# A retention layer whose gate, query and key features are made in pairs by seven block products

## The reference

```
h = rms_norm(x, norm_mix_g[1]);  proj = h @ w_in            # 1024 -> 2048 (q, k) + 2048 (v) + 2048 (g)
q = rotary(q), k = rotary(k) / 16                           # 4 heads of 256
s = (q k^T) * decay (causal);  ret = s @ v                  # v: 4 heads of 512
y = rms_norm(ret, out_g) * silu(g);  x = x + y @ w_out
```

## Time and profile before

| what | us |
|---|---|
| timed runs, median of 3 | 2112.48 (2112.15 to 2113.44) |
| the profiled execution, span of its instructions | 2111.6 |
| TensorE busy | 2094.3 |
| VectorE, ScalarE, GpSimd busy | 1358.7, 1088.4, 1115.7 |

### The profile page before, as it was taken

One profiled execution on the slowest core, in us unless ns is written; L12 is line 12 of the kernel. 1 busy time (PEld: TensorE's weight loads), 2 busy tenths in 40 slices (PEclk: granted clock), 3 DMA queues, 4 the chain that ended last, 5 costly groups with the idle time before them and its releaser, 6 DMA issues.

```text
span 2111.6 us, 29835 instructions
## 1 busy us (share of the span) xinstructions
PE 2094.3 (99%) x11235; PEld 1801.2 (85%) x11235; DVE 1358.7 (64%) x2284; ACT 1088.4 (52%) x1750; POOL 1115.7 (53%) x662
## 2 busy tenths in 40 slices
PE   9999999999999999999999999999999999999999
PEld 7867889889888888888899898888888888899998
DVE  7973786767634445467776684897567325785773
ACT  6564654654433424346546545445877535645642
POOL 3514666874534343435758834655433554838843
PEclk9999999999999999999999999999999999999999
DMA  4203223333322222222232324322212342333232
GB/s 167 70 11 93 97 92 100 101 101 106 119 85 90 85 91 84 92 80 89 92 101 93 117 85 174 110 80 72 78 61 71 91 140 90 100 100 101 90 108 93
DMA packets 57677, 200.69 MB, mean 95 GB/s; under 512 B 6400, under 2 KB 7168, under 8 KB 57280
## 3 DMA queue, kind: packets, MB, share of 16 engines
q1 hardware_dynamic: 56816, 197.46, 29.1%
q10 hardware_dynamic: 720, 1.34, 0.2%
HBM read 194.32 MB, written 4.19 MB: 94 GB/s over the span
## 4 chain that ended last, share of the span: by engine, by line
PE 91%; DVE 6%; issue 2%; ACT 2%; DMA 0%; SPq 0%; DVEq 0%; POOL 0%; ACTq 0%
PE ps L404 21%; PE ps L406 21%; PE ps L405 21%; PE ps L707 6%; PE ps L709 6%; PE ps L708 6%; PE ps L434 2%; PE ps L433 2%; PE ps L432 2%; PE ps L2444 1%; PE ps L1837 1%; DVE SC L1051 1%; DVE X L1024 0%; PE ps L2429 0%; PE ps L2456 0%
## 5 line engine op out<-in xcount | busy, mean ns | idle before, releaser
L382 POOL TENSOR_TENSOR WL<-WS,WH 128x1024 fp32r<-128x1024 f32 (+1 forms) x276 | 652.2, 2365 | 710.4 <-ACT WH L372 709.8
L404 PE MATMUL ps<-H,WH 128*128 128x512 f32 (+2 forms) x1488 | 580.8, 390 | 1.7 <-DVE H L612 1.1
L405 PE MATMUL ps<-H,WH 128*128 128x512 f32 (+2 forms) x1488 | 578.0, 388 | 0.0
L406 PE MATMUL ps<-H,WL 128*128 128x512 f32 (+2 forms) x1488 | 577.9, 388 | 0.0
L372 ACT ACTIVATE WH<-WS 128x1024 fp32r<-128x1024 f32 (+2 forms) x278 | 286.6, 1033 | 296.7 <-PE ps L406 167.1
L404 PEld LDWEIGHTS ps<-H,WH 128*128 128x128 f32 (+1 forms) x1488 | 279.1, 188 | 60.4 <-DVE H L612 2.7
L406 PEld LDWEIGHTS ps<-H,WL 128*128 128x128 f32 (+1 forms) x1488 | 279.0, 187 | 58.2
L405 PEld LDWEIGHTS ps<-H,WH 128*128 128x128 f32 (+1 forms) x1488 | 279.2, 188 | 54.5
L1213 POOL TENSOR_TENSOR WL<-WS,WH 128x512 fp32r<-128x512 f32 x162 | 214.2, 1333 | 197.1 <-ACT WH L830 195.3
L404 PE MATMUL ps<-G,WH 128*128 128x512 f32 x496 | 193.6, 390 | 2.0 <-DVE G L2163 1.4
L707 PE MATMUL ps<-G_long,WH 128*128 128x256 f32 x672 | 191.4, 285 | 2.6 <-DVE X L1024 2.1
(11 more groups left out here) (328 smaller groups left out, 4060.2 us busy)
## 6 DMA issues: line engine op xcount, KB each, us to landing
WS<-in_w SPq DMA_DIRECT2D x337, 512.0 KB, 3.5
WS<-in_w SPq DMA_DIRECT2D x24, 384.0 KB, 3.1
xs<-X SPq DMA_DIRECT2D x1, 2048.0 KB, 6.7
X<-xs SPq DMA_DIRECT2D x8, 256.0 KB, 3.7
out<-X SPq DMA_DIRECT2D x8, 256.0 KB, 2.0
X<-in_sg SPq DMA_DIRECT2D x1, 1344.0 KB, 6.0
X<-in_x ACTq DMA_DIRECT2D x4, 256.0 KB, 6.0
X<-in_x SPq DMA_DIRECT2D x4, 256.0 KB, 5.8
```

Of the source, the lines that this page charges most:

```text
L382: e.tensor_tensor(lo, raw, hi.bitcast(F), ALU.subtract).then_inc(*P.sig("w_lo", i))
L404: e.matmul(out, lh, rh, start=start, stop=False)
L405: e.matmul(out, lh, rl, start=False, stop=False)
L406: return e.matmul(out, ll, rh, start=False, stop=stop)
```

## The change

Of the retention's 32 gate, query and key features, 28 are made in pairs of seven products: 8 gate pairs, and the query pair and the key pair of heads 1 to 3. The query and key features of head 0 stay (units `bqk` 0, 1, 8, 9). Ahead of the heads, ScalarE scales X by the norm's weights, GpSimd makes the turned rows of the retention, ScalarE their high part and VectorE their low part. The scores stand around the pairs: two scores, the first gate pair, two scores, the second gate pair. ScalarE makes the forms' high parts, GpSimd the low parts; the weight sums are VectorE's for the gate and query pairs and GpSimd's for the key pairs.

```diff
+R_PAIRS = [("bg", i) for i in range(8)] + [("qk", i) for i in range(2, 8)]
...
-    for m in range(16):
+    for m in (0, 1, 8, 9):
...
-        u["bg", m] = [("b_w_in", 0, k, 4096 + 128 * m, 128) for k in K8]
+    for pair in R_PAIRS:
+        m1, m2 = (r_columns(pair) + 128 * z for z in range(2))
+        u["rp", *pair, 0] = [("b_w_in", 0, k, c, 128) for c in (m1, m2) for k in range(0, 8, 2)]
+        u["rp", *pair, 1] = [("b_w_in", 0, k, c, 128) for c in (m2, m1) for k in range(1, 8, 2)]
...
+def pe_row_pair(P, e, pair, amid=None, hold=False):
...
+    left, right, chain = a[:, 0:256], a[:, 256:512], b[:, 0:256]
+
...
+    pe_product(P, e, pair, "a11", "w_lo", chain, rows(0, 0), True)
+    if pair == ("bg", 0):
+        e.wait_ge(*P.at("t_lo", ("r", 3)))
+    pe_product(P, e, pair, "s1", "w_lo", right, turned("t1"), True)
+    e.wait_ge(*P.at("ct", (pair, "p1")))
+    pe_product(P, e, pair, "s2", "w_lo", chain, turned("t2"), False)
+    e.wait_ge(*P.at("ct", (pair, "p5")))
+    pe_product(P, e, pair, "a12", "w_lo", left, rows(1, 0), False)
+    if amid:
+        amid()
+    e.wait_ge(*P.at("ct", (pair, "u2")))
+    pe_product(P, e, pair, "s3", "w_lo", chain, turned("t3"), False)
+    pe_product(P, e, pair, "s4", "w_lo", right, rows(1, 1), False)
+    e.wait_ge(*P.at("c22", pair))
+    pe_product(P, e, pair, "a22", "w_lo", chain, turned("t4"), False)
+    P.cell_n += 1
+
+
...
-            feature(P, e, ("bg", 4 * h + j), P.hs())
+            if j % 2:
+                pe_row_pair(P, e, ("bg", 2 * h + j // 2))
...
+            q, k = (("qk", 2 * (h + 1) + part) for part in range(2))
+            pe_row_pair(P, e, q, row, True)
+            pe_row_pair(P, e, k)
+            for key in r_keys(q):
+                drop(P, key)
...
     e.preload_act_table_set("natural_log_exp_and_others")
     act_row_split(P, e, "nm1", 7)
-    qk_casts(0, 0)
+    cast(("bqk", 0))
+    cast(("bqk", 1))
     act_row(P, e, "nm1")
+    scaled(0)
+    scaled(1)
     qk_split(0, 0)
-    qk_casts(0, 1)
+    cast(("bqk", 8))
+    turned_hi(0)
+    scaled(2)
+    cast(("bqk", 9))
+    turned_hi(1)
+    scaled(3)
...
+    turned_hi(2)
+    turned_hi(3)
...
+        forms(one, "a11", "s1", "s2", "a12")
...
+        forms(one, "s3")
+        decayed(h, 0)
+        part(one, "p1")
+        forms(one, "s4")
+        decayed(h, 1)
+        part(one, "p5")
+        forms(one, "a22")
+        part(one, "u2")
+        forms(two, "a11", "s1", "s2")
+        silu(h, 0)
+        forms(two, "a12")
+        silu(h, 1)
+        forms(two, "s3")
+        decayed(h, 2)
+        part(two, "p1")
+        decayed(h, 3)
+        forms(two, "s4")
+        part(two, "p5")
+        forms(two, "a22")
+        part(two, "u2")
+        if h < 3:
+            forms(q, "a11", "s1", "s2", "a12")
+        silu(h, 2)
+        silu(h, 3)
+        if h < 3:
+            forms(q, "s3", "s4")
...
+        if h < 3:
+            part(q, "p1")
         act_row_split(P, e, name, 3, 2.0)
-        cast(("bqk", 2 * (h + 1)) if h < 3 else ("bout", 2, 1))
-        act_row(P, e, name, False)
         if h < 3:
-            cast(("bqk", 2 * (h + 1) + 1))
...
+            part(q, "p5")
+            forms(q, "a22")
+            part(q, "u2")
+            forms(k, "a11", "s1")
+            act_row(P, e, name, False)
+            forms(k, "s2", "a12")
+            y_high(h, 0)
+            forms(k, "s3")
+            part(k, "p1")
+            y_high(h, 1)
+            forms(k, "s4")
+            part(k, "p5")
+            y_high(h, 2)
+            forms(k, "a22")
+            part(k, "u2")
+            y_high(h, 3)
+            hi_to(P, e, P.ahead(("bout", h, 0)))
...
+        else:
+            cast(("bout", 2, 1))
+            act_row(P, e, name, False)
+            for i in range(4):
+                if i == 2:
+                    cast(("bout", 2, 2))
+                y_high(h, i)
             cast(("bout", 2, 3))
...
+def row_sum(P, e, pair, name):
...
+        e.wait_ge(*P.at(*P.raw_in(pair, 0)))
+        e.wait_ge(*P.at(*P.raw_in(pair, 1)))
+        t = e.tensor_tensor(dst, a21, a22, ALU.add)
+    elif name == "s3":
+        t = e.tensor_tensor(dst, a11, a21, ALU.subtract)
+    elif name == "s2":
+        e.wait_ge(*P.at(r_made(pair), (pair, "s1")))
+        t = e.tensor_tensor(dst, r_sum(P, pair, "s1"), a11, ALU.subtract)
+    else:
+        e.wait_ge(*P.at(r_made(pair), (pair, "s2")))
+        e.wait_ge(*P.at("w_lo", (pair, "a11")))
+        t = e.tensor_tensor(dst, a12, r_sum(P, pair, "s2"), ALU.subtract)
+    t.then_inc(*P.sig(r_made(pair), (pair, name)))
+
...
+    def right(pair):
+
+        x, y = (P.ps(key) for key in r_keys(pair))
+        e.wait_ge(*P.at("prod", (pair, "s3")))
+        e.tensor_tensor(y[:, 256:512], y[:, 0:256], r_s5(P, pair), ALU.add).then_inc(*P.sig("c22", pair))
+
+    def upper(pair):
+
+        x, y = (P.ps(key) for key in r_keys(pair))
+        e.wait_ge(*P.at("prod", (pair, "s4")))
+        e.tensor_tensor(x, x, r_part(P, pair), ALU.add).then_inc(*P.sig("c11", pair))
...
+    def sums(pair):
+
+        if pair[0] == "bg" and pair[1] % 2:
+            for name in ("s1", "s2"):
+                e.wait_ge(*P.at("w_lo", (("bg", pair[1] - 1), name)))
+        for name in ("s1", "s3", "s2"):
+            row_sum(P, e, pair, name)
...
+        decayed(h, 0)
+        decayed(h, 1)
+        sums(two)
+        right(one)
+        upper(one)
+        gate(h, 0)
+        row_sum(P, e, two, "s4")
+        gate(h, 1)
+        decayed(h, 2)
+        decayed(h, 3)
+        if h < 3:
+            sums(q)
+        right(two)
+        upper(two)
+        gate(h, 2)
+        if h < 3:
+            row_sum(P, e, q, "s4")
+        gate(h, 3)
...
+    def turned(q):
+
+        even, odd = r_scaled(P, q)[:, 0:T], r_scaled(P, q)[:, T:2 * T]
+        t1, t2, t3, t4 = (r_tx(P, q, 1, name, F) for name in ("t1", "t2", "t3", "t4"))
+        e.wait_ge(*P.at("t_eo", ("r", q, 1)))
+        e.tensor_tensor(t1, even[:, 256:512], even[:, 0:256], ALU.subtract).then_inc(*P.sig("t_part", ("r", q, 1)))
+        e.tensor_tensor(t3, odd[:, 256:512], even[:, 256:512], ALU.subtract).then_inc(*P.sig("t_part", ("r", q, 3)))
...
+    def units(key):
+        lo_to(P, e, P.index.get(key, 0) + 1)
+    for q, key in enumerate((("bqk", 8), ("bqk", 9), ("bv", 0, 0), ("bv", 0, 1))):
+        turned(q)
+        units(key)
+    for h in range(4):
+        units(("bv", h, 3))
+        for i in range(2):
+            low(("bg", 2 * h + i), "a11", "s1", "s2", "a12", "s3", "s4", "a22")
+        if h < 3:
+            q, k = ("qk", 2 * h + 2), ("qk", 2 * h + 3)
+            low(q, "a11", "s1", "s2", "a12", "s3", "s4")
+            e.wait_ge(*P.at("decay", (h, 3)))
+            for name in ("s1", "s3", "s2"):
+                row_sum(P, e, k, name)
+            low(q, "a22")
+            low(k, "a11")
+            row_sum(P, e, k, "s4")
+            low(k, "s1", "s2", "a12", "s3", "s4", "a22")
+            units(("bout", h, 0 if h == 2 else 3))
     lo_to(P, e, P.ahead(("bout", 3, 3), True))
 
 
...
-        e.wait_ge(*P.at(*(("decay", (h - 1, 3)) if h else ("g_lo", (0, FT - 1)))))
+        weights(("bqk", 9) if h == 0 else ("bout", h - 1, 0))
+        if h:
+            e.wait_ge(*P.at("k_sum", (("qk", 2 * h + 1), "s2")))
+            e.wait_ge(*P.at("w_lo", (("qk", 2 * h + 1), "s1")))
```

More of the change, by code:

```diff
@@ L324, in raw_ends @@
     key = P.order[i]
-    if key[0] not in ("dns", "ups"):
+    if key[0] not in PAIRED_UNITS:
         return [("w_lo", i)]
     pair, second = key[1:-1], key[-1]
+    if key[0] == "rp":
+        return [("w_lo", (pair, "a22" if second else "s4"))]
     if key[0] == "ups":
@@ L1538, in dve_ret @@
             add(2, 1, 1)
+        else:
+            right(q)
         dve_row(P, e, name, b, 0.0)
```

214 lines of the change are left out of this document (154 added, 60 removed).

## The result

| what | us |
|---|---|
| kernel before, median of 4 | 2112.32 (2112.15 to 2113.44) |
| changed kernel, median of 4 | 2131.7 (2130.8 to 2132.45) |
| ratio of the two | 1.0092, 95% interval 1.0077 to 1.0106 |
| span of the changed kernel's profiled execution | 2130.6 |

What follows compares the result with a forecast made beforehand. TensorE's work, plus whatever makes it wait, was taken as the bound. Savings of 11.9 us against waits and clock losses summed to +19.2 us, forecasting 2131.7 us, range 2118 to 2144.

Steps and rivals of the forecast that it cites:

- 14 pairs: Retention features made in pairs of 84 matmuls: 0.85 us of TensorE time saved each, 11.9 us in all.
- key feature 8: Start of retention: its GpSimd low part waits behind turned rows, whose scalings stand behind the row statistics; +10.1 us.
- third turn: Before the first value unit: GpSimd's turned rows wait for a ScalarE scaling behind a weight cast; +3.6 us.
- fourth turn: Among the values: the last turned rows and next low part take as long as a value unit; +0.5 us.
- c22: VectorE's addition before each first gate pair's last product, late through locks with GpSimd; 1.4 us each, +5.6 for four heads.
- end of the last head: Output unit (2,1) waits for a cast queued on ScalarE behind square, table load and split; +5.3 us.
- clock: TensorE drops to half rate behind three long waits, 1.7 us lost at each; +5.1 us.
- (a): Rival: waits at start and end come, but the first gate pair is not held; +12.7, or 2125 us; chance 0.22.
- (b): Rival: pairs lose more in ScalarE's single queue; +25.2, 2138 us, or 2143 with more slow clock; chance 0.14.
- (e): Rival: the clock also falls at the waits of 1.4 us; +26, or 2138.5 us; chance 0.06.
- (c): Rival: faster, as GpSimd's first turn finds its scalings early; -4.4, or 2108 us; chance 0.05.
- (d): Rival: no change, as (a) with a full clock and only the waits' lower bounds; +3.7, or 2116 us; chance 0.05.

Runs made afterwards that it cites:

- e1: Changed kernel with the first two turned rows' scalings moved ahead of the casts and row statistics on ScalarE: 2119.53 us.
- e2: Changed kernel with key feature 8's low part moved ahead of the first turned rows on GpSimd, each later turn one unit later: 2121.24 us.
- e4: Changed kernel with the last head's casts of output units (2,1) to (2,3) moved ahead of silu and the squares on ScalarE: 2123.21 us.
- e5: Changed kernel with the e3 move, the second pair's c22 one sum earlier, and its copies p5 and u2 earlier on ScalarE: 2127.23 us.
- e6: Changed kernel with 83 useless matmuls added to fill TensorE's three long pauses: 2126.82 us.
- e3: Changed kernel with the first gate pair's addition c22 behind one weight sum of the second pair, not three, on VectorE: 2132.18 us.
- e7: Changed kernel with the moves of e4 and e5, plus earlier scalings and low parts at the stage's start: 2105.11 us, ratio 0.997 to the kernel before.

## Why the prediction was right, point by point

Each term of the sum, as predicted and as the changed kernel's trace has it:

| term | predicted | measured |
|---|---|---|
| 14 pairs | -11.9 | -10.7 |
| query and key pairs late | +0.9 | in the line above |
| key feature 8 | +10.1 | +10.2 |
| third turn | +3.6 | +3.4 |
| fourth turn | +0.5 | 0 |
| c22, four heads | +5.6 | +5.0 |
| end of the last head | +5.3 | +5.3 |
| clock | +5.1 | +6.0 |
| sum | +19.2 | +19.2 |

- **Pairs.** From the first score of head 0 to its `ret` the kernel before takes 25.68 us:

```profile
593.70 0.39 PE L404 MATMUL ps<-G 128*128 128x512 f32 x1
...
619.38 0.39 PE L404 MATMUL ps<-G 128*128 128x512 f32 x1
```

  The changed kernel takes 25.24 for the same (611.38 to 636.62), with c22's 1.24 in it. So two gate pairs save 1.68, or 0.84 each, close to the 0.85 of the prediction and more than the 0.76 against a feature of 5.44 (10.88 - 10.12): the retention's own four gate features and their scores run a little above it. Four heads give 6.7 and three times 22.32 - 20.98 = 1.34 give 4.0, together 10.7. Predicted were 11.9 - 0.9 = 11.0. The mechanism is right, and nearly its size.
- **Key feature 8.** 571.37 - 560.73 = 10.64, against 0.47 before. The chain is the predicted one in each step, and e1 and e2 show it from both ends.
- **Third turn.** 3.26 us idle, 3.4 from start to start. It stayed in e1, as its own step says.
- **Fourth turn.** Predicted 0.5, seen as 0; this step is half right. The wait exists: e4, e5 and e6 each show 0.9 for the same low part, with a full clock there. In the changed kernel the matmuls ran at half rate in that place and lost the time themselves. The two terms overlap, and my sum added them.
- **c22.** The wait is there in all four heads, 1.24 each against 1.4. The lock did what the step says: each of the three sums took some 1.78 us, against 0.68 for such a sum while GpSimd was idle (the first row). VectorE, in the changed kernel:

```profile
604.61 0.68 DVE L1638 TENSOR_TENSOR SQ<-WS 128x512 f32<-128x512 f32 x1
...
618.04 1.78 DVE L1638 TENSOR_TENSOR SQ<-WS 128x512 f32<-128x512 f32 x1
619.75 1.78 DVE L1640 TENSOR_TENSOR WS<-WS 128x512 f32<-128x512 f32 x1
621.45 1.77 DVE L1643 TENSOR_TENSOR SQ<-SQ,WS 128x512 f32<-128x512 f32 x1
623.15 0.42 DVE L1669 TENSOR_TENSOR ps<-ps,rows_whole_G 128x256 f32<-128x256 f32 x1
```

  What the step did not see is that c22 was not alone. e3 took it away and gained nothing: the second pair's copies p1 and p5 kept their own time, and TensorE, now 1.2 us earlier, waited for them. Calling c22 the cause of 5.0 us would have been wrong by the counterfactual, though right as a reading of who releases whom.
- **End of the last head.** The last matmul ahead of the unit starts at 920.14 and takes 0.11 to the next, so the unit could start at 920.25; its second half starts at 931.79, 11.54 us later, against 912.32 - 908.12 = 4.20 before. Of the 7.34 more, 2.0 are the clock's. e4 removed the wait with one move.
- **Clock.** Key features 8 and 9 took 584.19 + 0.23 - 571.37 = 13.05 for 10.88; the values 611.38 - 587.84 = 23.54 for 21.76; the 12 matmuls from 926.58 to 931.33 took 4.75 for 2.72: 2.2 + 1.8 + 2.0 = 6.0. I had carried over 1.7 from one stretch; where the clock was low from the first matmul on, it cost 2.2 and 2.0, and 1.8 where it fell later. By the Trainium skill's page "TensorE: Matmul & The Clock Gate", section "Why this matters for your kernels", a pause between bursts brings half rate. Behind the pauses of 10.0 and 6.2 us the traces agree (0.50), and so does e6: with the pauses filled, the clock is 1.00. For pauses of 3.3 us and less the traces agree only in part (last section).
- **Rivals.** (a) fell, since c22 waited in each head; (b) since query and key pairs lost little; (e) since the granted clock was 1.00 behind c22 in all four heads (623.6 to 627, 721 to 725, 818.5 to 823, 899.6 to 905). For (c) GpSimd's turn would have had to be early, which it was not; (d) needed c22 in time and a clock that stays full, and neither came.

The measured terms add to 19.2, the spans differ by 19.0. That the sum met them to 0.2, and the median to the digit, is partly luck: the clock was 0.9 too small and the pairs' net saving 0.3 too large, against c22 with 0.6 and the fourth turn with 0.5 too much. No term was off by as much as 1 us, so the mechanism does not rest on this. The low stretch at 118 is in both traces, and their difference is free of it.

## What to carry to other kernels

When a faster form of the work asks the side engines for new operands, write for each new operation what stands ahead of it and behind it on its in-order engine, and who waits for those: here 10.7 us were saved and 29.9 lost, at four places in queues and by the clock that fell with them, and moving a few lines gave most of it back: 6.7 us of gain are left in e7. Before a wait is called a cause, look for what else is due within a microsecond of it on the other engines; removing the named releaser may only show the next (e3). And before a difference of medians is put down to a move, read in the trace the stretch that the move touches. A pause of TensorE as long as those of 6.2 and 10.0 us here costs its length and then about two more.
